# Value projections with x stationary and the weights streaming, two heads at a time

## The chip, the cores and the metric

The kernel runs on one core of a Trainium2 chip. The metric is the device time of one launch in microseconds (us), the median of the runs; lower is better. TensorE (PE) multiplies: it loads a stationary operand of 128 columns (its loads are listed as PEld) and streams a moving operand of up to 512 columns past it into PSUM. VectorE (DVE) and ScalarE (ACT) do the elementwise work, GpSimd (POOL) and SyncE (SP) mostly start transfers.

## What is computed

Two transformer layers run one after the other on 256 tokens of width 2048, in float32. The first has 16 "forgetting" softmax heads of 128 and a convolutional feed-forward part; the second has 4 heads of gated linear attention (GLA, keys of 128, values of 256) and 8 dilated softmax heads of 128, and a gated feed-forward part. Cut to the projections:

```
q, k, v, f_logit = jnp.split(h @ w_in, [hd, 2 * hd, 3 * hd], axis=-1)
q = rms_norm(q.reshape(bsz, seq, N_HEADS, HEAD_DIM), q_gain)
k = rms_norm(k.reshape(bsz, seq, N_HEADS, HEAD_DIM), k_gain)
s = jnp.einsum('bqhd,bshd->bhqs', qb, k) * scale + (cq - ck)
p = jax.nn.softmax(jnp.where(allowed, s, -jnp.inf), axis=-1)
out = jnp.einsum('bhqs,bshd->bqhd', p, v)
# second layer: qa, ka, va, ra, ga, qb, kb, vb = split(rms_norm_2(x) @ w_in)
attn = jnp.where(causal, einsum('bhnid,bhnjd->bhnij', q_t, k_t), 0.0)
o_intra = einsum('bhnij,bhnjv->bhniv', attn, vc)
chunk_state = einsum('bhncd,bhncv->bhndv', k_dec, vc)
```

So both kinds of head use v with its tokens as the contraction, that is, on the partitions.

## The kernel before

All weights arrive as 784 units of 512 KB, in the order in which they are used, through a ring of four buffers (`raw`). ACT rounds a unit to `whi` (float32r, L714), DVE takes the rest as `wlo` (L1038), three units ahead of their use (`AHEAD`). The activations stand in `xs` as a high and a low half in the same way. A unit holds 8 blocks of 128x128. For each block TensorE runs two matmuls: `whi` stationary with both halves of `xs` moving, 512 columns (L391, "hi"), and `wlo` stationary with the high half moving, 256 columns (L394, "lo"). Both add into one PSUM bank `acc`; DVE folds the two halves of the bank (`fold`, L1044) and scales them with `rstd` of the token (`take`, L1078). One chunk of 128 outputs takes two units, and comes out with features on the partitions and tokens along the row.

`stretch` writes the blocks in groups (4, 6, 6, 2 and so on): all hi matmuls of a group and then its lo ones. The order on every engine is written out by hand. `head` issues a softmax head: q into bank 1, k into bank 2, v into bank 3, six units in all; between them stand the attention steps of earlier heads: `head_values` (L453 to L455, two heads back), `head_scores` (one head back), `head_turn`. Since v must have its tokens on the partitions, `head_scores` begins with two transposes of `v_t` into the bank `b_val` (L439), and ACT copies them to `v_tok` (L745). A GLA head (`gla_head`) has twelve units: q, k, two chunks of v, two of the gate r. `gla_turn_v` transposes `g_v` in four pieces (L490), ACT copies them to `g_vtok` (L809), and only then `gla_chunk_states` (L498) can run. `b_val` also holds the transposed outputs of a GLA head (`gla_turn_out`, L510), read by DVE at L1192, which raises `g_gated`.

Waits are semaphores: `chunk_out` counts chunks that DVE has taken, `lo_ready` units that are split, `unit_used` units that TensorE is done with, `qk_rstd` and `qk_ready` the norm of q and k. A matmul that opens a bank waits for the `chunk_out` of the chunk that the bank held before.

In memory, the sizes of the tensors place every `whi` and `wlo` 128 bytes past a multiple of 256 in its partition, and `xs`, `mix` and `hid2` (the moving operands) 192 bytes past one.

Of the kernel before, what the change touches and what calls it, by code (L numbers as in the profile page):

```python
# [27 lines left out]
F32R = mybir.dt.float32r  # L28
# [6 lines left out]
P = 128  # L35
# [8 lines left out]
X_AT = 192  # L44
UW = BLOCKS * P
# [54 lines left out]
def build(nc, wstream, narrow_w, xt, vectors, identity, dist_onehot, rel_bias, gate_w2, scan_keep, gla_mask, fox_mask, out):  # L100
    with ExitStack() as ctx:
# [8 lines left out]
        whi = [sb(f"whi{i}", [P, UW], F32R) for i in range(RING)]  # L110
        wlo = [sb(f"wlo{i}", [P, UW], F32R) for i in range(RING)]
# [51 lines left out]
        v_t = put("v_t", [P, S])  # L163
        v_tok = put("v_tok", [P, 2, P])
# [26 lines left out]
        g_v = put("g_v", [P, 2, S])  # L191
# [29 lines left out]
        b_mean, b_score, b_turn, b_val = bank("b_mean"), bank("b_score"), bank("b_turn"), bank("b_val")  # L221

# [17 lines left out]
        v_turned, v_ready, scores_ready = sem("v_turned"), sem("v_ready"), sem("scores_ready")  # L240
# [6 lines left out]
        g_vturned, g_v_ready, g_cs, g_states, g_out = sem("g_vturned"), sem("g_v_ready"), sem("g_cs"), sem("g_states"), sem("g_out")  # L247
# [123 lines left out]
        def _(pe):  # L371
# [5 lines left out]

            def stretch(pos, blocks, x, *sizes):
# [3 lines left out]
                for size in sizes:  # L382
                    for k, j, bank_no, kc, opens, closes, free, late in blocks[at:at + size]:
# [4 lines left out]
                        if late:  # L388
                            pe.wait_ge(*late)
                        w_hi = whi[pos.slot(k)][:, j * P:(j + 1) * P]  # L390
                        pe.matmul(acc[bank_no][:, :], w_hi, x[:, kc, :, :].rearrange("p a s -> p (a s)"), start=opens, stop=False)  # L391
                    for k, j, bank_no, kc, opens, closes, free, late in blocks[at:at + size]:
                        w_lo = wlo[pos.slot(k)][:, j * P:(j + 1) * P]
                        mm = pe.matmul(acc[bank_no][:, S:2 * S], w_lo, x[:, kc, 0, :], start=False, stop=closes)  # L394
# [4 lines left out]
            def half(pos, k, bank_no, part, x, late=None):  # L399
                stretch(pos, unit_blocks(k, bank_no, part, None, late), x, BLOCKS)  # L400

# [48 lines left out]
            def head_values(h, means):  # L450
                pe.wait_ge(probs_t_ready, h + 1)
                pe.wait_ge(qk_rstd, means)
                pe.matmul(b_mean[:, 0:P], v_tok[:, 0, :], probs_t[:, 0:P], start=True, stop=True)  # L453
                pe.matmul(b_mean[:, P:S], v_tok[:, 0, :], probs_t[:, P:S], start=True, stop=False)  # L454
                pe.matmul(b_mean[:, P:S], v_tok[:, 1, :], probs_t[:, S:3 * P], start=False, stop=True).then_inc(head_ready, 1)  # L455
# [1180 lines left out]
```

## Time and profile before

| | us |
|---|---|
| median of the runs | 2256.49 |
| runs | 2256.23, 2256.49, 2273.54 |
| the profiled execution | 2258.64 |
| its span in the profile | 2256.9 |
| TensorE busy | 2242.0 (99%) |
| VectorE busy | 1617.8 (72%) |
| ScalarE busy | 1226.5 (54%) |

A row of a timeline gives the start, the time from the first start to the last end of a merged run of equal instructions, the engine, the line, the operation, what it writes and reads, and how many were merged; a wait stands in brackets with what ended it. Matmuls overlap in the pipe: what one of them takes of TensorE's time is the distance from its start to the start of the next, not its own duration. A row of groups gives the count, the busy time, the mean ns of one, and the idle time before. A row of waits gives who waited for whom, the us in total, how often, and the longest. A row by stretches gives the window, its length, and for each engine the busy time and (the count), then TensorE's granted clock as a share of the full one, the share of the DMA engines and GB/s.

### The profile page before, as it was taken

The page shows a single profiled execution, that of the slowest core. Times are in us where ns is not written, and L with a number is a line of the kernel's source. Part 1 is how long each engine was busy: PE and PEld are TensorE (multiplying, and loading weights), DVE is VectorE, ACT ScalarE, POOL GpSimd, SP SyncE. Part 2 cuts the span into 40 slices and gives each one's busy share as a digit, 9 for nine tenths or more (in the row PEclk, how much of TensorE's full clock was granted, in tenths as well). Part 3 has the DMA queues.
Part 4 walks back from the last instruction along what each step waited for, and adds up shares of the span by engine and source line. Part 5 has one row for each costly group of instructions (what it writes and reads, how often), then busy time and mean ns, then how long its engine had stood idle before and what let it go on. Part 6 is the DMA issues. An engine that isn't in the chain of part 4 may idle for free.

```text
span 2256.9 us, 38996 instructions
## 1 busy us (share of the span) xinstructions
PE 2242.0 (99%) x13138; PEld 1968.6 (87%) x13138; DVE 1617.8 (72%) x2394; ACT 1226.5 (54%) x1614; POOL 52.0 (2%) x78
## 2 busy tenths in 40 slices
PE   7999999999999999999999999999999999999999
PEld 6888888888888888888888888888888888888888
DVE  7877777788888888555567687777666666764554
ACT  6777765655555555444465577655444444443333
POOL 1111100000000000000000000000000000000000
PEclk9999999999999999999999999999999999999999
DMA  5555555555555555555545554455555555556564
GB/s 206 193 174 183 184 176 186 187 195 187 193 196 189 192 186 187 205 192 190 195 162 186 169 174 167 171 186 193 191 192 189 193 195 191 190 191 201 205 198 137
DMA packets 118598, 421.92 MB, mean 187 GB/s; under 512 B 13773, under 2 KB 15973, under 8 KB 118544
## 3 DMA queue, kind: packets, MB, share of 16 engines
q1 hardware_dynamic: 113760, 413.19, 53.8%
q0 software_dynamic: 2048, 5.42, 1.0%
q10 hardware_dynamic: 2736, 2.58, 0.4%
q8 instruction: 35, 0.57, 0.1%
q14 instruction: 19, 0.16, 0.0%
HBM read 419.01 MB, written 3.70 MB: 187 GB/s over the span
## 4 chain that ended last, share of the span: by engine, by line
PE 98%; DVE 1%; ACT 0%; DMA 0%; issue 0%; SPq 0%; DVEq 0%
PE acc L391 63%; PE acc L394 31%; PE b_score L442 0%; PE b_turn L447 0%; DMA xres<-xt 0%; PE b_mean L453 0%; PE b_mean L432 0%; PE b_mean L433 0%; PE b_val L439 0%; PE b_mean L455 0%; PE b_mean L454 0%; PE b_score L441 0%; ACT xs L842 0%; DVE wlo L1038 0%; DVE sq_all L1303 0%
## 5 line engine op out<-in xcount | busy, mean ns | idle before, releaser
L714 ACT ACTIVATE whi<-raw 128x1024 fp32r<-128x1024 f32 x783 | 825.8, 1058 | 821.4 <-PE acc L394 815.4
L1038 DVE TENSOR_TENSOR wlo<-raw,whi 128x1024 fp32r<-128x1024 f32 x783 | 959.5, 1229 | 389.3 <-ACT whi L714 386.6
L391 PE MATMUL acc<-xs,whi 128*128 128x512 f32 x4344 | 1130.7, 394 | 2.2 <-DVE wlo L1038 1.8
L391 PEld LDWEIGHTS acc<-xs,whi 128*128 128x128 f32 x4344 | 765.0, 188 | 124.7 <-DVE wlo L1038 2.9
L394 PEld LDWEIGHTS acc<-xs,wlo 128*128 128x128 f32 x4344 | 608.3, 188 | 64.8
L394 PE MATMUL acc<-xs,wlo 128*128 128x256 f32 x4344 | 620.3, 277 | 0.0
L391 PE MATMUL acc<-hid,whi 128*128 128x512 f32 x1408 | 359.9, 391 | 0.0
L1044 DVE TENSOR_REDUCE folded_t<-acc 128x256 f32<-128x512 f32 x336 | 231.4, 689 | 121.8 <-PE acc L394 110.2
L391 PEld LDWEIGHTS acc<-hid,whi 128*128 128x128 f32 x1408 | 247.2, 188 | 37.9
L394 PEld LDWEIGHTS acc<-hid,wlo 128*128 128x128 f32 x1408 | 194.2, 188 | 19.9
L394 PE MATMUL acc<-hid,wlo 128*128 128x256 f32 x1408 | 197.5, 276 | 0.0
L391 PE MATMUL acc<-mix,whi 128*128 128x512 f32 x512 | 131.5, 393 | 0.0
L391 PEld LDWEIGHTS acc<-mix,whi 128*128 128x128 f32 x512 | 90.4, 188 | 14.9 <-DVE mix L1136 0.5
L394 PEld LDWEIGHTS acc<-mix,wlo 128*128 128x128 f32 x512 | 70.6, 188 | 6.9
L394 PE MATMUL acc<-mix,wlo 128*128 128x256 f32 x512 | 71.9, 277 | 0.0
L830 ACT ACTIVATE hid<-hid 128x256 f32 (+1 forms) x88 | 36.2, 411 | 45.1 <-DVE hid L1265 44.9
L1104 DVE SCALAR_TENSOR_TENSOR qk_n<-qk,qk_gain,rstd_qk 128x256 f32<-128x256 f32 x48 | 21.6, 492 | 44.6 <-ACT rstd_qk L741 44.6
L1078 DVE TENSOR_TENSOR up_g<-folded_t,rstd 128x256 f32<-128x256 f32 x88 | 37.5, 426 | 3.0
L1078 DVE TENSOR_TENSOR up_v<-folded_t,rstd 128x256 f32<-128x256 f32 x88 | 37.5, 426 | 3.0
L1269 DVE TENSOR_TENSOR hid<-hid,hid 128x256 f32 (+1 forms) x88 | 36.9, 419 | 1.0 <-ACT hid L830 1.0
L815 ACT ACTIVATE tap_g<-up_g,vec 128x256 f32<-128x256 f32 x44 | 26.5, 603 | 16.2 <-DVE up_g L1078 16.1
L823 ACT ACTIVATE tap_v<-up_v,vec 128x256 f32<-128x256 f32 x44 | 26.5, 603 | 15.2 <-DVE up_v L1078 15.1
(195 smaller groups left out, 998.8 us busy)
## 6 DMA issues: line engine op xcount, KB each, us to landing
raw<-wstream SPq DMA_DIRECT2D x783, 512.0 KB, 3.3
decay_row<-decay_scratch POOLq DMA_DIRECT2D x16, 128.0 KB, 3.5
out<-xres ACTq DMA_DIRECT2D x16, 128.0 KB, 2.9
xres<-xt SPq DMA_DIRECT2D x3, 512.0 KB, 8.7
dist_scratch<-bias_scratch POOLq DMA_DIRECT2D x8, 192.0 KB, 4.7
toeplitz<-dist_scratch POOLq DMA_DIRECT2D x8, 128.0 KB, 3.3
xres<-xt SPq DMA_DIRECT2D x2, 256.0 KB, 4.6
raw<-wstream SPq DMA_DIRECT2D x2, 256.0 KB, 5.7
```

What stands on the lines that cost most here:

```text
L391: pe.matmul(acc[bank_no][:, :], w_hi, x[:, kc, :, :].rearrange("p a s -> p (a s)"), start=opens, stop=False)
L394: mm = pe.matmul(acc[bank_no][:, S:2 * S], w_lo, x[:, kc, 0, :], start=False, stop=closes)
L714: act.activation(whi[slot][:, :], raw[slot][:, :], ACT.Copy).then_inc(hi_ready, 1)
L815: act.activation(tap_g[:, :], up_g[:, 0:S], ACT.Identity, scale=column("conv0", j), bias=column("convb", j)).then_inc(tap0, 1)
L823: act.activation(tap_v[:, :], up_v[:, 0:S], ACT.Identity, scale=column("conv0", FC + j), bias=column("convb", FC + j)).then_inc(tap0, 1)
L830: act.activation(hid2[:, j, 0, :], hid[:, :], ACT.Copy).then_inc(hid_hi_ready, 1)
L1038: dve.tensor_tensor(wlo[slot][:, :], raw[slot][:, :], whi[slot][:, :], ALU.subtract).then_inc(lo_ready, 1)
L1044: dve.tensor_reduce(folded_t[0:rows, :], acc[bank_no][0:rows, :].rearrange("p (a s) -> p s a", a=2), AX_X, ALU.add).then_inc(chunk_folded, 1)
L1078: dve.tensor_tensor(dst, folded_t[0:rows, :], rstd[0:rows, :], ALU.mult).then_inc(chunk_out, 1)
L1104: dve.scalar_tensor_tensor(out=qk_n[:, a, :], in0=qk[:, a, :], scalar=qk_gain[:, col + a:col + a + 1], in1=rstd_qk[:, a, :], op0=ALU.mult, ...
L1269: dve.tensor_tensor(hid2[:, j, 1, :], hid[:, :], hid2[:, j, 0, :], ALU.subtract).then_inc(hid_split, 1)
```

## The change

The value projections swap the roles of their operands. A weight unit of values now holds 4 pieces of 256 columns (two softmax heads, or one GLA head, side by side) for 4 rows of blocks. A block is one of two 128-token halves of `xs`: its high half is stationary with the 256 columns of `whi` and of `wlo` moving, 512 columns in two runs that lie 16 KB apart (L406 of the new kernel), and its low half is stationary with `whi` moving, 256 columns (L413). Even blocks add into bank 3, odd ones into a second bank, `b_val` (bank 0 for GLA). The values come out with tokens on the partitions.

```diff
+        w = sb("w", [P, 2, RING, UW], F32R)
+        whi = [w[:, 0, i, :] for i in range(RING)]
+        wlo = [w[:, 1, i, :] for i in range(RING)]
...
+            def value_blocks(k, v, even, odd, free=None):
+                return [(k, j, (even, odd)[j % 2], (4 * v + j // 2, j % 2), v == 0 and j < 2, v == 3 and j >= 6,
+                         free if v == 0 and j == 0 else None, None) for j in range(BLOCKS)]
+            def value_parts(pos, k, j, x, kc):
+                tokens, cols = slice(kc[1] * P, (kc[1] + 1) * P), slice(j // 2 * S, (j // 2 + 1) * S)
+                return x[:, kc[0], 0, tokens], x[:, kc[0], 1, tokens], w[:, :, pos.slot(k), cols], w[:, 0, pos.slot(k), cols]
...
+            def rstd_columns(n, tile):
+                pe.wait_ge(rstd_ready, n + 1)
+                for t in range(2):
+                    mm = pe.matmul(tile[:, 2 * S - 2 + t:2 * S - 1 + t], rstd[0:1, t * P:(t + 1) * P], one[0:1, :], start=True, stop=True)
+                mm.then_inc(rstd_turned, 1)
...
             def head_scores(h):
                 pe.wait_ge(qk_ready, 2 * h + 2)
-                for t in range(2):
-                    mm = pe.transpose(b_val[:, t * P:(t + 1) * P], v_t[:, t * P:(t + 1) * P], ident[:, :])
-                mm.then_inc(v_turned, 1)
...
-            def head_values(h, means):
+            def head_values(h, means, j, taken):
+                v = slice(j * P, (j + 1) * P)
+                pe.wait_ge(chunk_out, taken)
...
-                units(8, 10, 4, 6, 6)
-                gla_turn_v(g, True)
-                units(10, 11, 4, 4)
+                units(8, 11, 4, 6, 6, 4, 4)
...
+                    elif not j:
+                        pe.wait_ge(chunk_out, chunk)
+                        pe.wait_ge(g_gated, GLA_HEADS)
...
-            def copy_v(n):
-                act.wait_ge(v_turned, n + 1)
-                act.activation(v_tok[:, :, :].rearrange("p a s -> p (a s)"), b_val[:, 0:S], ACT.Copy).then_inc(v_ready, 1)
...
+            def take_values(dst, banks, last_unit, chunk, layer):
+                dve.wait_ge(unit_used, last_unit + 1)
+                dve.wait_ge(rstd_copied, layer)
+                for t in range(2):
+                    fold(P, banks[t], chunk + t)
+                    dve.tensor_scalar(dst[:, t, :], folded_t[:, :], rstd_col[:, t:t + 1], None, ALU.mult).then_inc(chunk_out, 1)
...
                 if s == 0 and lag >= 1:
-                    take(v_t[:, :], 3, pos.unit(k0 - 1), run.chunk0 + 3 * h - 1)
+                    if not j:
+                        take_values(v_tok, (3, 4), pos.unit(k0 - 1), pair - 2, 1 if run.kind == "fox" else 2)
                     norm_qk(run, n - 1)
...
-                if s == 6:
-                    take(g_v[:, 0, :], 3, chunk(2), L1.chunk_heads + 6 * g + 2)
...
-                    take(g_v[:, 1, :], 1, chunk(3), L1.chunk_heads + 6 * g + 3)
+                    take_values(g_vtok, (3, 0), chunk(3), L1.chunk_heads + 6 * g + 2, 2)
```

The units keep their number, their size and their places; only what the value units hold is rearranged, on the host. The values of both heads of a pair are taken together, after the second head. Since a token's scale now belongs to a partition, `rstd` is turned into two columns once per layer (`rstd_columns`: two matmuls of one row and one column, and a copy by DVE). In memory, `whi` and `wlo` have become one tensor `w` that starts 224 bytes past a multiple of 256; `xs` is still at 192.

On TensorE, inside the loop over softmax heads, where a new head has issued its two q units (`b_mean` is the bank of the head outputs, `b_score` that of the scores). Before:

```order
L453 MATMUL b_mean<-probs_t,v_tok 128x128 [waits qk_rstd,probs_t_ready]
L454 MATMUL b_mean<-probs_t,v_tok 128x128
L455 MATMUL b_mean<-probs_t,v_tok 128x128
L439 MATMUL b_val<-ident,v_t 128x128 [waits qk_ready]
L439 MATMUL b_val<-ident,v_t 128x128
L441 MATMUL b_score<-qk_n 128x128
L442 MATMUL b_score<-qk_n 128x256
L385 REGISTER_ALU
L391 MATMUL acc<-xs,whi 128x512 [waits chunk_out,lo_ready]
```

After:

```order
L483 MATMUL b_mean<-probs_t,v_tok 128x128 [waits qk_rstd,probs_t_ready,chunk_out]
L484 MATMUL b_mean<-probs_t,v_tok 128x128
L485 MATMUL b_mean<-probs_t,v_tok 128x128
L469 MATMUL b_score<-qk_n 128x128 [waits qk_ready]
L470 MATMUL b_score<-qk_n 128x256
L399 REGISTER_ALU
L409 MATMUL acc<-xs,w 128x512 [waits chunk_out,lo_ready]
```

The two transposes are gone, and the head's values now wait for `chunk_out` as well.

On VectorE, where a new pair of heads begins (`folded_t` is the folded bank, `qk_n` the normed q and k). Before, for every head:

```order
L1038 TENSOR_TENSOR wlo<-raw,whi 128x1024 [waits hi_ready]
L1043 ISA [waits unit_used]
L1044 TENSOR_REDUCE folded_t<-acc 128x256 [waits chunk_out]
L1046 REGISTER_ALU
L1078 TENSOR_TENSOR v_t<-folded_t,rstd 128x256 [waits chunk_folded]
L1104 SCALAR_TENSOR_TENSOR qk_n<-qk,qk_gain,rstd_qk 128x256 [waits qk_rstd]
L1104 SCALAR_TENSOR_TENSOR qk_n<-qk,qk_gain,rstd_qk 128x256
L1037 REGISTER_ALU
L1038 TENSOR_TENSOR wlo<-raw,whi 128x1024 [waits hi_ready]
```

After, for every second head:

```order
L1065 TENSOR_REDUCE folded_t<-acc 128x256 [waits chunk_out,rstd_copied,unit_used]
L1111 TENSOR_SCALAR v_tok<-folded_t,rstd_col 128x256 [waits chunk_folded]
L1065 TENSOR_REDUCE folded_t<-b_val 128x256 [waits chunk_out]
L1111 TENSOR_SCALAR v_tok<-folded_t,rstd_col 128x256 [waits chunk_folded]
L1136 SCALAR_TENSOR_TENSOR qk_n<-qk,qk_gain,rstd_qk 128x256 [waits qk_rstd]
L1136 SCALAR_TENSOR_TENSOR qk_n<-qk,qk_gain,rstd_qk 128x256
L1059 TENSOR_TENSOR w<-raw,w 128x1024 [waits hi_ready]
```

One fold and one scaling for each head have become two and two for each pair, both ahead of the norm of q and k; the new ones write `v_tok` itself.

On TensorE, in the first dilated head, with the banks' numbers: the last unit of k and the first units of v. Before:

```order
L391 MATMUL acc2<-xs,whi3 128x512 [waits lo_ready]
L391 MATMUL acc2<-xs,whi3 128x512 x7
L394 MATMUL acc2<-xs,wlo3 128x256 x8
L391 MATMUL acc3<-xs,whi0 128x512 [waits lo_ready,chunk_out]
L391 MATMUL acc3<-xs,whi0 128x512 x7
L394 MATMUL acc3<-xs,wlo0 128x256 x8
L391 MATMUL acc3<-xs,whi1 128x512 [waits lo_ready]
```

After:

```order
L409 MATMUL acc2<-xs,w 128x512 [waits lo_ready]
L409 MATMUL acc2<-xs,w 128x512 x7
L416 MATMUL acc2<-xs,w 128x256 x8
L406 MATMUL acc3<-w,xs 128x512 [waits lo_ready,g_gated,chunk_out]
L406 MATMUL b_val<-w,xs 128x512
L406 MATMUL acc3<-w,xs 128x512
L406 MATMUL b_val<-w,xs 128x512
L406 MATMUL acc3<-w,xs 128x512
L406 MATMUL b_val<-w,xs 128x512
```

The first value matmul now waits for `g_gated` too, because `b_val`, its second bank, still holds the last GLA head's output until DVE's L1192 has read it.

## Rows read from the trace of the kernel before

**Rows 1.** The page: span, engines, and the chain that ended last.

```profile
span 2256.9 us, 38996 instructions
PE 2242.0 (99%) x13138; PEld 1968.6 (87%) x13138; DVE 1617.8 (72%) x2394; ACT 1226.5 (54%) x1614; POOL 52.0 (2%) x78
...
PE 98%; DVE 1%; ACT 0%; DMA 0%; issue 0%; SPq 0%; DVEq 0%
```

**Rows 2.** The waits of TensorE, the longest and the fourth of six.

```profile
PE acc L606 <- DVE wlo L1287: 7.4, 1, 7.4
...
PE b_mean L432 <- DVE sq_lo L1083: 0.6, 1, 0.6
```

**Rows 3.** Groups by line, shapes apart, TensorE.

```profile
L391 PE MATMUL acc<-xs,whi 128*128 128x512 f32 x4344 | 1130.7, 394 | 2.2 <-DVE wlo L1038 1.8 <-DVE xs L1061 0.4
L394 PE MATMUL acc<-xs,wlo 128*128 128x256 f32 x4344 | 620.3, 277 | 0.0
...
L439 PE MATMUL b_val<-ident,v_t 128*128 128x128 f32 x48 | 9.3, 275 | 0.0
...
L490 PE MATMUL b_val<-ident,g_v 128*128 128x128 f32 x16 | 2.4, 272 | 0.0
```

**Rows 4.** Timeline of TensorE inside one softmax head.

```profile
275.35 0.84 PE L394 MATMUL acc<-xs,wlo 128*128 128x256 f32 x6
276.03 1.54 PE L391 MATMUL acc<-xs,whi 128*128 128x512 f32 x6
277.40 0.84 PE L394 MATMUL acc<-xs,wlo 128*128 128x256 f32 x6
```

**Rows 5.** Timeline of TensorE where a head's scores are issued.

```profile
271.68 0.38 PE L439 MATMUL b_val<-ident,v_t 128*128 128x128 f32 x2
271.90 0.39 PE L441 MATMUL b_score<-qk_n 128*128 128x128 f32 x2
...
273.49 0.63 PE L394 MATMUL acc<-xs,wlo 128*128 128x256 f32 x4
273.96 0.40 PE L391 MATMUL acc<-xs,whi 128*128 128x512 f32 x1
```

**Rows 6.** Timeline of TensorE around the value transposes of a GLA head.

```profile
1245.45 0.60 PE L490 MATMUL b_val<-ident,g_v 128*128 128x128 f32 x4
1245.81 1.18 PE L391 MATMUL acc<-xs,whi 128*128 128x512 f32 x4
1246.82 0.62 PE L394 MATMUL acc<-xs,wlo 128*128 128x256 f32 x4
```

**Rows 7.** Timeline at the first dilated head.

```profile
1301.36 0.87 DVE L1192 SCALAR_TENSOR_TENSOR g_of<-b_val,vec,g_silu 128x256 f32<-128x256 f32 x2
...
1301.79 2.00 PE L391 MATMUL acc<-xs,whi 128*128 128x512 f32 x8
```

**Rows 8.** Timeline where a new pair of softmax heads begins.

```profile
284.23 0.69 DVE L1044 TENSOR_REDUCE folded_t<-acc 128x256 f32<-128x512 f32 x1 [0.87 <-PE acc L394]
...
287.25 0.88 DVE L1104 SCALAR_TENSOR_TENSOR qk_n<-qk,qk_gain,rstd_qk 128x256 f32<-128x256 f32 x2 [1.87 <-ACT rstd_qk L741]
...
289.95 0.38 PE L453 MATMUL b_mean<-probs_t,v_tok 128*128 128x128 f32 x2
```

**Rows 9.** Timeline where the output projection of the first layer begins.

```profile
322.00 0.69 DVE L1044 TENSOR_REDUCE folded_t<-acc 128x256 f32<-128x512 f32 x1 [0.77 <-PE acc L394]
...
322.73 0.42 DVE L1078 TENSOR_TENSOR v_t<-folded_t,rstd 128x256 f32<-128x256 f32 x1
...
325.13 0.88 DVE L1104 SCALAR_TENSOR_TENSOR qk_n<-qk,qk_gain,rstd_qk 128x256 f32<-128x256 f32 x2 [1.98 <-ACT rstd_qk L741]
...
325.24 0.46 PE L453 MATMUL b_mean<-probs_t,v_tok 128*128 128x128 f32 x2
```

**Rows 10.** Engines in two stretches: two forgetting heads, one GLA head.

```profile
252.08:290.00 37.92, 37.92 (x229) 33.58 (x228) 29.71 (x55) 27.07 (x42) 5.29 (x10) 1.00 0.54 183
...
1208.14:1245.46 37.32, 37.32 (x220) 32.65 (x219) 25.32 (x42) 20.90 (x26) 1.61 (x3) 1.00 0.55 179
```

More of the change, by code:

```diff
@@ L109, in build @@
         raw = [sb(f"raw{i}", [P, UW]) for i in range(RING)]
-        whi = [sb(f"whi{i}", [P, UW], F32R) for i in range(RING)]
-        wlo = [sb(f"wlo{i}", [P, UW], F32R) for i in range(RING)]
+        rstd_col = sb("rstd_col", [P, 2])
+        one = sb("one", [P, 1])
+        sb("skipped_w", [P, (W_AT - nc.sbuf_base) % PHASE // 4])
+        w = sb("w", [P, 2, RING, UW], F32R)
+        whi = [w[:, 0, i, :] for i in range(RING)]
+        wlo = [w[:, 1, i, :] for i in range(RING)]
         xres = sb("xres", [P, KC, S])
@@ L547, in project @@
                 stretch(pos, units(0, 0, 1, {0: (mix_ready, last - 1)}), mix, 4, 4)
-                head_values(last - 1, last + 1)
+                head_values(last - 1, last + 1, 0, layer.chunk_out)
                 head_scores(last)
@@ L615, in _ @@
             half(first, 3, 2, 1, xs)
-            half(first, 4, 3, 0, xs)
+            value_half(first, 4, 0, 3, 4)
             norm_mean(0)
@@ L619, in _ @@
             distance_biases()
-            half(first, 5, 3, 1, xs)
+            value_half(first, 5, 1, 3, 4)
             half(first, 6, 0, 0, xs)
             half(first, 7, 0, 1, xs)
-            pe.wait_ge(rstd_ready, 1)
+            pe.wait_ge(chunk_out, 1)
+            rstd_columns(0, b_turn)
             head_mean(0)
@@ L630, in _ @@
             head_scores(0)
-            pe.wait_ge(chunk_out, FOX.chunk0 + 3)
-            half(first, 10, 3, 0, xs)
-            half(first, 11, 3, 1, xs)
+            value_half(first, 10, 2, 3, 4)
+            value_half(first, 11, 3, 3, 4)
             head_turn(0)
@@ L1147, in head_step @@
                         dve.wait_ge(qk_ready, 2 * n)
-                    take(qk[:, 0, :], 1, pos.unit(k0 + 1), run.chunk0 + 3 * h)
+                    take(qk[:, 0, :], 1, pos.unit(k0 + 1), pair + 2 * j)
                     if lag >= 1:
@@ L1157, in head_step @@
                 if s == 4:
-                    take(qk[:, 1, :], 2, pos.unit(k0 + 3), run.chunk0 + 3 * h + 1)
+                    take(qk[:, 1, :], 2, pos.unit(k0 + 3), pair + 2 * j + 1)
                 if s == 5:
@@ L1165, in tail_step @@
                 if s == 0:
-                    take(v_t[:, :], 3, unit0 - 1, run.chunk0 + 3 * run.n - 1)
+                    take_values(v_tok, (3, 4), unit0 - 1, run.chunk0 + 3 * run.n - 2, 1 if run.kind == "fox" else 2)
                     norm_qk(run, n - 1)
@@ L1359, in first_fox_heads @@
                 square_low(0, 1)
-                take(v_t[:, :], 3, pos.unit(5), FOX.chunk0 + 2)
+                rstd_columns(1, b_turn)
                 split(10)
@@ L1562, in units_in, with units_values, units_pairs @@
     return a.reshape(-1, P, BLOCKS, P)
+def units_values(w):
+    return w.reshape(4, 4, P, 2 * P).transpose(0, 2, 1, 3).reshape(4, P, BLOCKS, P)
+def units_pairs(w, q, k, v, heads):
+    each, values = units_in(w, [c + h for h in range(heads) for c in (q, k)]).reshape(heads, 4, P, BLOCKS, P), []
+    for i in range(heads // 2):
+        u = units_values(w[:, (v + 2 * i) * P:(v + 2 * i + 2) * P])
+        values += [each[2 * i], u[:2], each[2 * i + 1], u[2:]]
+    return np.concatenate(values)
 def units_out(w):
@@ L1591 @@
     hd = FOX_HEADS * P
-    fox_order = [FOX_HEADS * part + h for h in range(FOX_HEADS) for part in range(3)]
     w1 = a["fox_w_in"][0]
```

112 lines of the change are left out of this document (63 added, 49 removed).

## The prediction

> **What bounds the kernel now.** I read the page first, then the waits of TensorE, then the groups by line, and last the timeline at the places that the change touches. The page shows TensorE busy for 2242.0 of 2256.9 us, and 98% of the chain that ended last is TensorE's [rows 1]. Its waits are few and lie at the start: the longest is 7.4 us for the first split, and one of 0.6 us for `sq_lo` stands before the first `head_mean` [rows 2]. So time is won by what leaves TensorE's stream, and lost by what enters it or makes it wait. DVE and ACT have room: in 37.92 us of two softmax heads DVE is busy 29.71 and ACT 27.07, in 37.32 us of a GLA head 25.32 and 20.90 [rows 10]. Work that only they gain or lose costs nothing unless TensorE comes to wait for it.
>
> What one matmul takes is read from starts. Six lo matmuls go from 275.35 to 276.03, 113 ns each; six hi ones from there to 277.40, 228 ns each [rows 4]. A block is 342 ns. Their own durations, 277 and 394 ns [rows 3], overlap and are no price.
>
> **The value matmuls.** There are 24 softmax heads with 2 units of values and 4 GLA heads with 4: 64 units, 512 blocks, 175 us at 342 ns. Afterwards there are as many blocks, with one load of 128 columns and 512 moving columns, one load and 256 columns, in groups of the same sizes. So the swap in itself removes no matmul. Two things in it are new. The first is that the 512 moving columns are two runs of 256. No row has such a pattern. At the low end each run costs what a 256-column matmul of its own costs, 2 x 113 = 226 ns [rows 4], 2 ns less than now: 512 x 2 = 1 us gained. At the high end I use a slower tempo that the trace knows: after the fp32 matmuls of the scores four lo matmuls go from 273.49 to 273.96, 118 ns each [rows 5]. With two runs at 118 a hi matmul would be 236 ns, 8 more, and the lo one 5 more: 512 x 13 = 6.7 us lost. I take 0, since the columns and their order within a run are the same and the row of the 256-column matmuls is the nearest. The second is that `xs` is loaded as weights and `w` streams, while DVE and ACT write other slots of `w`; they write `whi` and `wlo` today beside every load without any wait of TensorE [rows 2]. I take 0 again.
>
> **What leaves TensorE.** Two transposes per softmax head: the first of the pair starts at 271.68, the scores at 271.90, so 0.22 us [rows 5]. With 24 heads, 48 instructions [rows 3], 24 x 0.22 = 5.3 us. In a GLA head four of them run from 1245.45 to 1245.81, 0.36 us, and the four hi matmuls behind them, to 1246.82, take 1.01 where 4 x 0.228 = 0.91 would do, since their first one still waits for the last transpose in the pipe: 0.10 more [rows 6]. 4 x 0.46 = 1.8 us. Together **7.1 us** for 64 transposes.
>
> Here a rule of the Trainium skill stands against the rows. Its page "TensorE: Matmul & The Clock Gate", in the section "Part 4: PE-mode transpose", gives about 275 ns for a 128x128 transpose in a kernel's context. The trace agrees for the duration of one (272 and 275 ns), and shows about 110 from one start to the next. By the page's figure the 64 would be 17.6 us, and the sum would be 2239 us instead of the one below; this is a rival.
>
> **What enters TensorE.** The two `rstd_columns`, two small fp32 matmuls each. No row has one of one column; above, each costs no more than a transpose of 128 columns, 0.11 us [rows 5], 0.2 us per place; below, nothing. The first place lies inside the 0.6 us wait for `sq_lo` [rows 2], the second stands in the stream: I take 0.2 us, and up to 0.2 more. `head_values` gets a wait for `chunk_out` and one register instruction to compute it; I take nothing, because such instructions stand before most groups today without a wait in the rows.
>
> **New waits.** In the first dilated head the first value matmul waits for `g_gated`. It is due at 1301.79, but DVE's L1192 runs from 1301.36 for 0.87 us, to 2.23 [rows 7]. TensorE waits about **0.5 us**, once; all that is queued behind it, the other value blocks and the `head_mean` of that head, comes later by as much, and since TensorE sets the end, so does the end.
>
> The other waits are for the values. In the loop DVE folds at 284.23; the norm of q and k can start only at 287.25, when `rstd_qk` is there [rows 8]. A fold and its scaling take from 322.00 to 323.15, 1.15 us [rows 9]; two pairs take 2.3 us and end at 286.5, 0.7 us before DVE can go on anyway. The head's values on TensorE are due at 289.95 [rows 8], 3.4 us after. The tightest place is the start of the output projection, where only one unit lies between: DVE folds at 322.00, would be done at 324.3, and the norm starts at 325.13, just ahead of the values at 325.24 [rows 9], which wait for the same `rstd_qk`. So the cover is 0.8 us there. If it went, TensorE would wait for the rest of the second pair, at most 1.1 us at each of 12 pairs. In a GLA head the two pairs come where one is now, two units further on than a fold that goes away; their reader, `gla_chunk_states`, follows three units later (8 us). What ACT no longer does, 28 copies, hides behind TensorE and brings nothing.
>
> **The sum.** The profiled execution took 2258.64 us, 1.7 more than its span and 2.1 more than the median. 2258.6 - 7.1 + 0.5 + 0.2 = 2252.2; against the median, 2256.5 - 6.4 = **2250 us**, 0.3% less.
>
> **Rivals.**
>
> *Every matmul becomes slower (slower than before).* The change also moves the weights of all 6264 blocks [rows 3] from 128 to 224 bytes past a multiple of 256. If a load then takes longer, the lo matmul, which has the least time to hide the next load, shows it first. For it: lo matmuls do run at 118 instead of 113 in places [rows 4, 5], so something other than their 256 columns can hold them. Against it: no row ties that to an address. Price: 5 ns for each block would be 6264 x 5 = 31 us, less those that are slow today; with some 6000 it is 30, and 2250 + 30 = 2280 us. It decides from about 1 ns per block, 6.4 us, where the gain is gone. The same page, section "LDWEIGHTS (loading the stationary operand)", gives a load as its columns over 1.2 GHz, 107 ns for 128; by it a lo matmul, 113 ns here, has hardly any room for a longer load. It states nothing on addresses, and no row here shows that a load sets this pace.
>
> *The two runs cost something (no change).* The high end above: +6.7, so 2256 to 2257 us, with the transposes paid back. For it, the pattern is new to this kernel; against it, its reads are still whole runs of 1 KB.
>
> *TensorE waits for the values.* The wait of the transposes is replaced by one for DVE: 12 x 1.1 = 13 us at most, 2263 us. Against it stand covers of 0.7 us and more at DVE and 3.4 us at TensorE [rows 8, 9].
>
> *Transposes cost their whole duration, or the new placement helps.* By [rows 3] 48 x 0.275 + 16 x 0.272 = 17.6 us: 2258.6 - 17.6 + 0.7 gives 2242 for the profiled execution, 2239 or 2240 against the median. Against it, the rows of starts. A placement that took 2 ns from each hi matmul would give 6264 x 2 = 13 us: 2237 us. Nothing in the rows asks for it.
>
> **Chances.** Forecast 0.66 (its own range 2245 to 2255: the tempo after fp32 matmuls, 113 or 118, varies between heads, and 0.15 us for each of 24 heads is 4 us); two runs dearer 0.12; waits for values 0.05; all matmuls slower 0.10; cheaper in one of the last two ways 0.07. The range reaches from 2240 to 2270: it holds the forecast, the dearer runs and the waits, and the lower half of the slower matmuls; it leaves out some 0.06 on each side. A change of 1% (23 us, below 2234 or above 2279) is about what a measurement can tell from none. Faster by more has 0.03, slower by more 0.06, within it 0.91.
>
> **What would show it right or wrong.** Starts of six hi matmuls of values 1.37 us apart as a group, and six lo ones 0.68: the swap is free. No row with `v_t` or `g_v`, and the scores right behind the head's values: the transposes are gone, 0.22 us a head. One wait of TensorE for DVE's `g_of` near 0.5 us: the new wait. No waits of TensorE for `v_tok` or `g_vtok`: the cover holds. The q and k groups, and the feed-forward parts that the change does not touch, at 1.37 and 0.68 as now: if these are longer, the first rival holds, and the prediction is wrong by tens of us.

## The result: 2% slower, in all matmuls on the streamed weights

The changed kernel takes 2306.92 us (median; 2306.75 to 2308.92) where the kernel before, run beside it, takes 2257.39: a ratio of 1.0187, with a 95% interval of 1.0137 to 1.0236. The forecast was 2250. The profiled execution took 2306.75 us and has a span of 2305.0, 48.1 more than before. Executions of one and the same kernel can differ by steps of some 13 us (the kernel before: 2256 to 2260, 2270 to 2274, seldom 2283), and the last section of the experiments follows one such step in two profiles.

The page of the changed kernel, the lines that answer to [rows 1]:

```profile
span 2305.0 us, 38875 instructions
PE 2289.7 (99%) x13082; PEld 1996.3 (87%) x13082; DVE 1619.4 (70%) x2397; ACT 1217.9 (53%) x1586; POOL 52.0 (2%) x78
...
PE 98%; ACT 1%; DMA 1%; DVE 1%; issue 0%; SPq 0%; DVEq 0%
```

TensorE has 56 matmuls fewer and is busy 47.7 us longer. Its waits, the view of [rows 2]:

```profile
PE acc L629 <- DVE w L1321: 7.1, 1, 7.1
PE acc L409 <- DVE w L1059: 1.8, 1, 1.8
PE b_mean L463 <- DVE sq_lo L1115: 1.1, 1, 1.1
...
PE acc L406 <- issue: 0.3, 1, 0.3
```

None of them is new and long. So the 48 us are in the stream itself. Where [rows 4] and [rows 5] were read, two q and k groups, a value group and the scores now stand like this on the timeline of TensorE:

```profile
271.22 0.39 PE L484 MATMUL b_mean<-probs_t,v_tok 128*128 128x128 f32 x2
271.44 0.39 PE L485 MATMUL b_mean<-probs_t,v_tok 128*128 128x128 f32 x2
271.66 0.39 PE L469 MATMUL b_score<-qk_n 128*128 128x128 f32 x2
271.89 0.60 PE L470 MATMUL b_score<-qk_n 128*128 128x256 f32 x2
...
275.84 1.56 PE L409 MATMUL acc<-xs,w 128*128 128x512 f32 x6
277.23 0.88 PE L416 MATMUL acc<-xs,w 128*128 128x256 f32 x6
277.95 0.39 PE L406 MATMUL acc<-w,xs 128*128 128x512 f32 x1
...
279.35 0.28 PE L413 MATMUL acc<-w,xs 128*128 128x256 f32 x1
...
280.05 0.39 PE L406 MATMUL acc<-w,xs 128*128 128x512 f32 x1
```

Six hi matmuls of q and k take 277.23 - 275.84 = 1.39 us, six lo ones 0.72 (before 1.37 and 0.68 [rows 4]); six value ones 1.40 and 0.70. The lo matmuls, at 120 ns instead of 113, are the clearest sign. The slower pace is also where the change altered nothing. In the feed-forward part of the first and of the second layer, TensorE's matmuls in 300 us, first before, then after (window, length, busy and count, clock, DMA share, GB/s):

```profile
600.00:900.00 300.00, 300.00 (x1755) 1.00 0.56 191
1800.00:2100.00 300.00, 300.00 (x1755) 1.00 0.57 195
```

```profile
600.00:900.00 300.00, 300.00 (x1705) 1.00 0.56 186
1800.00:2100.00 300.00, 300.00 (x1706) 1.00 0.56 187
```

A block is two matmuls: 300 / 877.5 = 341.9 ns before, 300 / 852.5 = 351.9 after, at the same granted clock (1.00, the level of 2.4 GHz). (A window also counts the matmuls that its two ends cut, so these figures are 0.3 ns low in a window of 300 us; from start to start they are 342.2 and 352.2.)

Now all starts of the two traces, with each block compared with the block of the same unit. The 5760 blocks that kept their form (the first unit's included) went from 231.2 to 234.2 ns behind a hi matmul and from 115.1 to 120.8 behind a lo one, 8.7 ns a block and 49.9 us in all. The 512 value blocks went from 350.0 to 355.2 ns, 2.7 us. All other matmuls, the transposes among them, take 71.9 us before and 67.6 after (4.2 less, unrounded), and the first matmul starts 0.3 us earlier. 49.9 + 2.7 - 4.2 - 0.3 = 48.1, the whole difference of the spans.

### The profile page after: what moved, and what is told of

Its sections match the earlier page's. It is cut to its first block, busy times and chain, and to the rows that moved or that the text cites. A ratio compares the mean times of both kernels' runs of the same rounds, so it can differ in the third digit from the quotient of the medians.

```text
span 2305.0 us, 38875 instructions
## 1 busy us (share of the span) xinstructions
PE 2289.7 (99%) x13082; PEld 1996.3 (87%) x13082; DVE 1619.4 (70%) x2397; ACT 1217.9 (53%) x1586; POOL 52.0 (2%) x78
## 4 chain that ended last, share of the span: by engine, by line
PE 98%; ACT 1%; DMA 1%; DVE 1%; issue 0%; SPq 0%; DVEq 0%
PE acc L409 58%; PE acc L416 30%; PE acc L406 3%; PE b_val L406 2%; PE acc L413 2%; PE b_val L413 1%; PE b_score L470 0%; PE b_turn L475 0%; DMA xres<-xt 0%; PE b_mean L463 0%; PE b_mean L483 0%; PE b_score L469 0%; PE b_mean L464 0%; PE b_mean L485 0%; PE b_mean L484 0%
## 5 line engine op out<-in xcount | busy, mean ns | idle before, releaser
L746 ACT ACTIVATE w<-raw 128x1024 fp32r<-128x1024 f32 x783 | 824.9, 1057 | 872.8 <-PE acc L416 827.5
L1059 DVE TENSOR_TENSOR w<-raw,w 128x1024 fp32r<-128x1024 f32 x783 | 959.3, 1228 | 419.8 <-ACT w L746 417.5
L409 PE MATMUL acc<-xs,w 128*128 128x512 f32 x3832 | 1005.0, 397 | 2.2 <-DVE w L1059 1.8
L409 PEld LDWEIGHTS acc<-xs,w 128*128 128x128 f32 x3832 | 680.4, 188 | 119.8 <-DVE w L1059 2.9
L416 PEld LDWEIGHTS acc<-xs,w 128*128 128x128 f32 x3832 | 548.2, 188 | 59.1
L416 PE MATMUL acc<-xs,w 128*128 128x256 f32 x3832 | 565.4, 282 | 0.0
L409 PE MATMUL acc<-hid,w 128*128 128x512 f32 x1408 | 364.9, 394 | 0.0
L409 PEld LDWEIGHTS acc<-hid,w 128*128 128x128 f32 x1408 | 249.2, 188 | 41.4
L416 PEld LDWEIGHTS acc<-hid,w 128*128 128x128 f32 x1408 | 200.6, 188 | 21.1
L416 PE MATMUL acc<-hid,w 128*128 128x256 f32 x1408 | 206.8, 283 | 0.0
L409 PE MATMUL acc<-mix,w 128*128 128x512 f32 x512 | 133.2, 396 | 0.0
L406 PE MATMUL acc<-w,xs 128*128 128x512 f32 x320 | 111.3, 401 | 0.3 <-issue 0.3
L409 PEld LDWEIGHTS acc<-mix,w 128*128 128x128 f32 x512 | 91.0, 188 | 16.0 <-DVE mix L1168 0.5
L416 PEld LDWEIGHTS acc<-mix,w 128*128 128x128 f32 x512 | 72.5, 188 | 7.3
L406 PE MATMUL b_val<-w,xs 128*128 128x512 f32 x192 | 75.9, 395 | 0.0
L406 PEld LDWEIGHTS acc<-w,xs 128*128 128x128 f32 x320 | 58.8, 188 | 10.2 <-issue 1.1
L413 PE MATMUL acc<-w,xs 128*128 128x256 f32 x320 | 67.6, 280 | 0.0
L413 PEld LDWEIGHTS acc<-w,xs 128*128 128x128 f32 x320 | 54.0, 188 | 5.5
```

The costliest lines, as they stand in the source:

```text
L406: pe.matmul(acc[bank_no][:, :].rearrange("p (a s) -> p a s", a=2), x_hi, w_both, start=opens, stop=False)
L413: mm = pe.matmul(acc[bank_no][:, S:2 * S], x_lo, w_hi, start=False, stop=closes)
L746: act.activation(whi[slot][:, :], raw[slot][:, :], ACT.Copy).then_inc(hi_ready, 1)
L1059: dve.tensor_tensor(wlo[slot][:, :], raw[slot][:, :], whi[slot][:, :], ALU.subtract).then_inc(lo_ready, 1)
```

## Experiments

What is common to q, k, output and feed-forward matmuls is where their weights lie. The theories (the expectations call form and rest together theory B):

- **Placement.** `w` at 224 instead of 128 (places are bytes past a multiple of 256) slows every matmul. Either its own place counts (A1), or the distance from the stationary to the moving operand (A2), or how ACT and DVE write into `w` while TensorE reads (A3).
- **Form.** The new value blocks, with two runs and alternating banks, leave the pipe in a slower state that lasts.
- **The rest.** The dropped transposes, the new tensors or semaphores change the pace.

From here on *distance* is the place of the moving operand minus that of the stationary one, modulo 256. Before it was 192 - 128 = 64 for every block. After it is 192 - 224 = 224 for the old blocks, and 224 - 192 = 32 for the value blocks, where the roles are swapped.

### The kernel before with its weights at 224

```diff
+        sb("pad_w", [P, 24])
         whi = [sb(f"whi{i}", [P, UW], F32R) for i in range(RING)]
         wlo = [sb(f"wlo{i}", [P, UW], F32R) for i in range(RING)]
+        sb("pad_x", [P, 40])
```

> The kernel before, with 96 bytes of padding ahead of the rounded weights, so that every whi and wlo starts 224 bytes past a multiple of 256 as in the changed kernel, and padding behind them so that xres and xs keep 128 and 192. Nothing else differs. Theory A (the start of the weights in the partition makes every block slower, wherever it is used): six hi and six lo matmuls take 2.10 us and more instead of 2.05, and the time is 2300 to 2315 us, since the changed kernel lost 50 us and saved some 6 elsewhere. Theory B (the swap of operands, the alternating banks or the new code slow TensorE down, the placement is innocent): 2257 us as before.

2313.5 us (2313.32 and 2313.67), ratio 1.0218 [1.0160, 1.0276]. Two empty tensors do it. Its groups of lo and hi in the second feed-forward part, and its matmuls in the same two windows:

```profile
1800.44 1.56 PE L393 MATMUL acc<-xs,whi 128*128 128x512 f32 x6
1801.83 0.88 PE L396 MATMUL acc<-xs,wlo 128*128 128x256 f32 x6
1802.55 0.62 PE L393 MATMUL acc<-xs,whi 128*128 128x512 f32 x2
```

```profile
600.00:900.00 300.00, 300.00 (x1705) 1.00 0.57 186
1800.00:2100.00 300.00, 300.00 (x1705) 1.00 0.58 187
```

1.39 and 0.72 us for six, and 1705 matmuls: the pace of the changed kernel, with no value block in it. Theories of form and of the rest fall as causes of the 48 us. The span is 2311.9, 55.0 above before and 6.9 above after. Run times alone would leave the ratio uncertain (the 13 runs of the kernel before beside it go from 2256.32 to 2283.28); the paces in the traces do not depend on that.

### The changed kernel with its weights at 128, and at 192

```diff
-        sb("skipped_w", [P, (W_AT - nc.sbuf_base) % PHASE // 4])
+        sb("skipped_w", [P, 48])
```

> The changed kernel with w at 128 past a multiple of 256, where whi and wlo stood before. Theory A: 2251 us, 6 less than before, because then only the forecast terms are left: 7.1 us for the transposes, 0.5 and 0.2 for the new wait and the columns. Theory B: near 2307, as the changed kernel. If the two runs of 256 moving columns cost something themselves, up to 7 us more than 2251.

2255.85 us (2254.46 to 2269.68, 10 runs), ratio 0.9982 [0.9952, 1.0013]. For the second, `skipped_w` is 64 columns, and `skipped` also, so that `xs` stays at 192:

> The changed kernel with w at 192, the place that the constant W_AT names. Theory A1 (a load is slow when it starts 32 bytes past a multiple of 64): as fast as with 128, 2251 us. Theory A2 (what counts is how the stationary and the moving operand stand to each other within 256 bytes: 64 apart before, 32 after): here they are 0 apart, and the time differs from that with 128 by more than 10 us, most likely upwards. Theory B: 2307.

2294.69 us (2293.76 to 2296.06), ratio 1.0135 [1.009, 1.018]. The two windows, at 128 and then at 192:

```profile
600.00:900.00 300.00, 300.00 (x1756) 1.00 0.59 190
1800.00:2100.00 300.00, 300.00 (x1757) 1.00 0.61 194
```

```profile
600.00:900.00 300.00, 300.00 (x1716) 1.00 0.58 187
1800.00:2100.00 300.00, 300.00 (x1715) 1.00 0.59 189
```

At 128, the place before, the loss of 48 us is gone, and the feed-forward blocks are at 341.6 ns again. The gain that was expected, down to 2251 us, does not come in full. At 192 (distance 0) a block takes 349.7. At 192 the value blocks run at the pace of the q and k blocks, 231.3 and 118.7 ns for both (median of the groups of six): two runs of 256 columns and two alternating banks cost nothing there. At 128 they run at 233.8 and 115.2, where the median group of the old blocks has 228.8 and 113.3; the swap of the roles turns their distance from 64 to 192. By these medians that would be 6.9 ns x 512 = 3.5 us, the price from which the experiment with the values at distance 64 starts. Start to start and unit by unit it is less: the value blocks took 350.0 ns in the kernel before, slower than its feed-forward blocks, and take 353.3 here, 3.3 more or 1.7 us.

### The kernel before with xs moved, alone and together with the weights

```diff
-X_AT = 192
+X_AT = 224
```

> The kernel before with the weights left at 128 and the moving operands xs, mix and hid2 at 224 past a multiple of 256. Theory A1, which is about loads only: 2257 us. A form of it in which any operand that starts 32 bytes past a multiple of 64 is slow: 2290 to 2310. Theory A2 (distance between the two, now 96): also slower, by an amount that it doesn't say. Theory B: 2257.

2321.48 us, ratio 1.0253 [1.0195, 1.0312]: distance 96, the slowest of all kernels here. The weights lie where they lay, and what ACT and DVE write into them is the same; A1, which is about the stationary operand's place, falls as the only cause, and A3 with it. Next, the weights at 224 as in the first experiment and `X_AT = 32`, so both lie 96 bytes on and the distance is 64 again:

> The kernel before with both moved by the same 96 bytes: weights at 224 past a multiple of 256, xs, mix and hid2 at 32 (224 + 64). Theory A2 (only the distance from the stationary to the moving operand counts, modulo 256 bytes): 2257 us, blocks at 228.8 and 113.3 ns, as before. Theory A1 (an operand 32 bytes past a multiple of 64 is slow by itself): 2310 us or more, since now both are. Theory A3 (it is the writes of ScalarE and VectorE to w, by their place, that hold TensorE): also about 2310, since the weights are where they were in the slow run.

2258.01 us (8 runs, 2256.31 to 2285.63) against 2258.84: 0.9997 [0.9950, 1.0043]. The windows of the second feed-forward part, distance 96 and then 64:

```profile
1800.00:2100.00 300.00, 300.00 (x1701) 1.00 0.57 186
```

```profile
600.00:900.00 300.00, 300.00 (x1721) 1.00 0.56 188
1800.00:2100.00 300.00, 300.00 (x1757) 1.00 0.60 193
```

352.7 ns a block against 341.5. The same `w` at 224 that cost 55 us costs nothing once `xs` goes along: it is the distance (A2). The 1721 in the first layer is taken up below.

### TensorE alone: maps of the distance

The first map holds only TensorE's blocks (six hi, six lo, four times) for all 64 pairs of places in steps of 32 bytes, on operands that nobody writes:

> No part of the reference is computed: after one load and one rounding, TensorE alone runs 64 stretches of 24 hi and 24 lo matmuls in groups of six, one for each pair of places (stationary and moving operand at 0, 32, ... 224 past a multiple of 256), with a small fp32 matmul between stretches; ScalarE, VectorE and the transfers rest. Theory A2: the pace depends on moving minus stationary alone, 228.8 and 113.3 ns at +64, 232.2 and 120.0 at -32, 231.3 and 118.7 at 0, 233.2 and 120.2 at +96, the same along each diagonal. Theory A1: rows and columns at 32, 96, 160, 224 are slow and the others fast. Theory A3: all 64 stretches run at 229 and 113, since nobody else touches the memory.

A group of hi and one of lo, stationary at 128, moving at 192 and then at 224:

```profile
394.00 1.55 PE L68 MATMUL acc<-x,w 128*128 128x512 f32 x6
395.38 0.87 PE L70 MATMUL acc<-x,w 128*128 128x256 f32 x6
396.09 0.40 PE L68 MATMUL acc<-x,w 128*128 128x512 f32 x1
...
402.54 1.57 PE L68 MATMUL acc<-x,w 128*128 128x512 f32 x6
403.94 0.52 PE L70 MATMUL acc<-x,w 128*128 128x256 f32 x3
```

1.38 us against 1.40 for the six hi ones, with all other engines idle: no other engine is needed for a difference. Neither map computes anything of the reference. The second map adds moving places up to 1 KB on, steps of 16 bytes, and the form of the value blocks with two alternating banks and with one:

> No part of the reference is computed: TensorE alone, as in the first map, but with the lo weights 16 KB behind the hi ones as in the kernel, the stationary operand at 128 and the moving one at 0 to 992 in steps of 32, then at 144 to 256 in steps of 16; then 8 stretches in the form of the values (tokens stationary at 192, two runs of 256 columns moving at 0 to 224, two banks in turn) and 8 of that form with one bank. Theory A2 with a period of 256 bytes: the four rounds of the first 32 repeat each other, the best is +64, and there the pace is 228.8 and 113.3. The value form: the same paces at the same distance, 228.8 and 113.3 for the moving operand at 0, 231.2 and 118.7 at 192, 233.8 and 115.2 at 128, with one bank as with two.

Mean distances of starts in ns, hi / lo, by the distance of the operands, the first group of each stretch left out; first map (mean of eight pairs), value form of the second map with two banks and with one (one pair each, the stationary at 192):

```
distance      0            32           64           96           128          160          192          224
first map     231.2/118.8  232.3/117.5  230.3/118.0  234.0/119.3  231.9/117.2  233.2/117.6  232.4/115.2  232.9/119.4
two banks     230.6/118.7  231.6/117.3  228.8/117.7  233.2/120.2  231.7/117.1  232.9/117.4  232.3/117.9  232.2/120.0
one bank      230.6/118.7  231.5/117.3  228.8/117.7  233.2/120.2  231.7/117.1  233.0/117.3  232.3/117.9  232.2/120.0
```

At six of the eight distances the pace repeats with 256 bytes: with the stationary at 128, moving places 192, 448, 704 and 960 (distance 64) all give 230.8 / 118.1, and 64, 320, 576 and 832 (distance 192) all give 232.5 / 114.2. The form of the value blocks costs nothing, and neither does their bank pattern: at the same pair of places, with the stationary at 192, the first map and the two value rows agree within 0.1 ns for hi and 0.3 for lo (moving at 0: 228.8 ns for hi in all three, so 230.3 in the table is the mean of unlike pairs). Distances 96 and 224 are worst, as in the kernels, with 353.3 to 353.6 and 352.1 to 352.4 ns a block in all eight pairs of each.

But the distance alone does not set the pace, as the expectation of the first map had it. Within one distance the pairs differ: a block takes 349.3 to 353.5 ns at distance 0, 346.7 to 349.0 at 64, 346.7 to 350.0 at 192. Nor do the two places settle it: the pair 128 and 160 stands twice in the second map, with 351.1 and 348.7, so what ran before counts too. And no block at distance 64 came near the 342.2 of the kernels; no group of lo matmuls reached 113.3 there. From 64 to 224 the maps have 3 to 6 ns a block, the kernels 10. The last experiment takes this up.

### Values at distance 64 too

Each slot of `w` is 64 columns longer, and value units are written and read 128 bytes on, so that their place is 0 and their distance 0 - 192 = 64:

```diff
+V_AT = 32
-        w = sb("w", [P, 2, RING, UW], F32R)
+        w = sb("w", [P, 2, RING, UW + 64], F32R)
...
-                act.activation(whi[slot][:, :], raw[slot][:, :], ACT.Copy).then_inc(hi_ready, 1)
+                act.activation(w[:, 0, slot, unit_at(pos.base + k)], raw[slot][:, :], ACT.Copy).then_inc(hi_ready, 1)
```

> The changed kernel with w at 128 and, in addition, the value units written 128 bytes further on in their slots, so that for values too the moving operand (w, at 0 modulo 256) stands 64 above the stationary one (xs, at 192). Theory A2 (only moving minus stationary counts): value groups of six fall from 233.8 and 115.2 ns (run with w at 128) to 228.8 and 113.3, 6.9 ns for each of 512 blocks, 3.5 us less than that run: 2251 us, 6 less than before. If the two runs of 256 columns or the alternating banks have a price of their own, the value groups stay above 229 and 113, and the time at 2254.

2268.18 us (2255.98 to 2283.21, 12 runs), ratio 1.0043 [1.0011, 1.0075]: not the gain of 3.5 us. Start to start the value blocks went from 353.3 to 352.0 ns, 1.3 less, 0.7 us in all (lo matmuls at 117.4, not 113.3), and the first layer's feed-forward part runs slow, the second's not:

```profile
600.00:900.00 300.00, 300.00 (x1722) 1.00 0.58 188
1800.00:2100.00 300.00, 300.00 (x1757) 1.00 0.60 194
```

### The transposes issued twice

```diff
-                for t in range(2):
+                for t in (0, 1, 0, 1):
```

in `head_scores` and, the same, in `gla_turn_v` of the kernel before: 64 more transposes (the repeated ones write the same results again).

> The kernel before with each of the 64 value transposes issued twice. By the distances between starts, 0.22 us a head and 0.45 us a GLA head, it takes 7.1 us more than before (64 x 0.11); by the rule of 275 ns for one, 17.6 us more.

2267.77 us (10 runs) where the kernel before beside it has a median of 2257.00, ratio 1.0016 [0.9987, 1.0045]. The 23 runs of the kernel before go from 2255.87 to 2283.62, so the times do not resolve 7 us; the traces do. The span is 2267.5, 10.6 above before. On the timeline:

```profile
51.00 0.60 PE L439 MATMUL b_val<-ident,v_t 128*128 128x128 f32 x4
51.43 0.39 PE L441 MATMUL b_score<-qk_n 128*128 128x128 f32 x2
```

Four take 0.43 us where two took 0.22 [rows 5]. Over all places, the time from the matmul ahead to the one behind grows from 342.3 to 560.5 ns in a softmax head and from 474.2 to 911.2 in a GLA head: 24 x 0.218 + 4 x 0.437 = 7.0 us, 109 ns each. The wait for `sq_lo` is 1.4 us longer, and most of the remaining 2 us are head blocks at a slower pace: of the groups of six lo matmuls in the first 330 us, 65 of 84 run near 118 ns, where in the kernel before it was 26 of 85. So the transposes' own price is that of the prediction, 7.1, and not 17.6.

### Two tempi at distance 64

Two profiles have a slow first layer: that of the kernel before with both operands moved, and that with the values at distance 64. The changed kernel with `w` at 128 was run once more, the same code:

> The changed kernel with w at 128 once more, for a closer ratio. If the change without its placement is worth the 2.7 us that the two profiled executions are apart: 0.9988 of the kernel before. If it is nothing: 1.000. A gain of 0.3% as forecast (0.997) needs the values' blocks to cost nothing, which the earlier run of it does not show (6.9 ns a block, 3.5 us).

2255.08 us (12 runs), ratio 0.9981 [0.9959, 1.0003]. This time the profiled execution was one of the longer ones, span 2267.6 against 2254.2:

```profile
600.00:900.00 300.00, 300.00 (x1724) 1.00 0.55 188
1800.00:2100.00 300.00, 300.00 (x1755) 1.00 0.56 194
```

348.0 ns a block in the first layer's feed-forward part (348.9 from start to start), where the earlier profile of this kernel has 341.7 (342.2). Laid side by side, the two traces are 0.3 us apart at 492 us and 13.4 at 1209, and from there to the end the difference stays 13.5. So at distance 64 there are two tempi, hi 228.9 / lo 113.3 and hi 230.8 / lo 118.1 ns (the next expectation leaves out the last matmul of each group and so has 228.4 and 231.2), and in these two traces the loop of the first feed-forward part keeps one of them throughout. Is that TensorE's own doing too?

> TensorE alone again, nothing of the reference is computed. At the distance of the kernel before (stationary 128, moving 192) the kernels' own traces show two tempi, hi 228.4 with lo 113.4 ns and hi 231.2 with lo 118 ns, and they go from the one to the other in the first half. Stretches of 60 to 160 groups of hi and lo matmuls: groups of six at that distance without a break, the same with the stationary at 224, with a 128-column matmul after every group, after every fourth, the same in float32, groups of 4, 6, 6, groups of 8, the stationary at 224 with a float32 matmul after every fourth, and the first one again. If the quick tempo is the state that an undisturbed stream finds and a break throws it out of it, the first and last stretch run at 228.4 and 113.4 after some groups, those with breaks at 231 and 118 for some groups behind each, and the stretches at 224 stay at 232 and 120 throughout. If the quick tempo needs the other engines' traffic, all stretches at 192 run at 230 and 118 as in the map of 64 combinations. If only float32 matmuls bring the slow tempo, the fifth stretch alone shows it.

TensorE alone at distance 64, in a long stretch of groups of six ahead and in one at the end that has the same instructions; between them a stretch at distance 224:

```profile
200.00:380.00 180.00, 180.00 (x1040) 1.00 0.00 1
420.00:500.00 80.00, 80.00 (x457) 1.00 0.00 1
...
1520.00:1660.00 140.00, 140.00 (x822) 1.00 0.00 1
```

From start to start a block takes 346.7 ns in the first (228.8 / 117.8), 342.2 in the last (228.9 / 113.3) and 352.2 at distance 224; the counts of such short windows would make it up to 2 ns less. No engine but TensorE is at work. The last stretch is quick from its first group, the first never becomes quick in its 160 groups. With a float32 matmul behind every fourth group, the tempo changes at the break:

```profile
889.36 0.87 PE L79 MATMUL acc<-x,w 128*128 128x256 f32 x6
890.07 0.38 PE L68 MATMUL mark<-xraw,wraw 128*128 128x128 f32 x2
...
891.68 0.84 PE L79 MATMUL acc<-x,w 128*128 128x256 f32 x6
892.36 1.54 PE L77 MATMUL acc<-x,w 128*128 128x512 f32 x6
...
898.52 0.38 PE L68 MATMUL mark<-xraw,wraw 128*128 128x128 f32 x2
...
900.13 0.87 PE L79 MATMUL acc<-x,w 128*128 128x256 f32 x6
900.84 1.55 PE L77 MATMUL acc<-x,w 128*128 128x512 f32 x6
```

Six lo matmuls take 0.71 us ahead of the first break, 0.68 behind it and 0.71 behind the next; two stretches at 118 and one at 113 follow each other regularly. With a 128-column matmul of the rounded operands as a break, all stay at 117 to 118. Groups of eight, without a break, alternate between 118 and 113, and those of 4, 6, 6 go three by three. At distance 224 float32 breaks never bring the quick tempo: 118 right behind one and 120 after it. So each of my expectations is wrong in part: the quick tempo needs no other engine, a stream of groups of six does not find it by itself, and more than float32 matmuls can change it. What went before sets the tempo; by what means is not shown, and what sets it in the kernel, ahead of the first layer's feed-forward part, is open.

This also splits the 10.0 ns that a feed-forward block lost in the changed kernel. At distance 64 a block takes 342.2 ns at the quick tempo and 348.9 at the slow one; at 224 it takes 352.2, and not one group of lo matmuls in the changed kernel is below 115 ns (889 of 1029 groups of four or more are in the kernel before). So 6.7 ns are the quick tempo, which distance 224 never showed, and 3.3 ns are what 224 costs on top of the slow one.

## Why the prediction was wrong, step by step

- **What bounds the kernel: right.** 98% of the chain is TensorE's, and what was slow was slow in its stream.
- **The pace of the blocks that keep their form: this step failed.** The sum has terms for transposes, columns and one wait, and leaves all other blocks at their old pace; the move of the weights from 128 to 224 stands in it at nothing, with no row that says so. The runs show 8.7 ns a block by all starts (10.0 in the feed-forward parts), 49.9 us: the distance between the operands went from 64 to 224. The placement stood among the rivals, with 0.10, and its price was too small, 5 ns a block and 31 us. I had priced the lo matmuls alone (5.7 by all starts), and the hi ones became 3.0 ns slower as well. The sign named for this rival, q and k groups and feed-forward parts longer than 1.37 and 0.68, is the one that came: 1.39 and 0.72. The mechanism that I gave it, a longer load by the weights' own place, is refuted: at the same 224 with `xs` at 32 nothing is lost. That lo matmuls run at 118 in places was rightly seen as a sign that something besides their columns holds them; it is the slow tempo of distance 64. The evidence against the rival, "no row ties that to an address", said that nothing was known, and I read it as a small chance. The range ended at 2270 for that reason.
- **The value blocks: nearly.** "Two runs cost nothing" is shown by the kernel at distance 0 and by the second map. "I take 0 again", for `xs` as weights and `w` streaming, is wrong by a little: it was argued from the writes of ACT and DVE and the absence of waits [rows 2], but the swap turns the distance round. Against the blocks of the same units before, that is 1.7 us with `w` at 128 and 2.7 us in the changed kernel itself.
- **The transposes: right.** No row of `v_t` or `g_v`, and the scores start 0.22 us behind the last matmul of the head's values. The doubled transposes measure 7.0 us for 64. By the Trainium skill, "TensorE: Matmul & The Clock Gate", section "Part 4: PE-mode transpose", a transpose takes about 275 ns, and an estimate by it for the doubling is 17.6 us; the trace agrees with the 275 as a duration (272 and 275 ns [rows 3]) and not as a price in a stream (109 ns).
- **`g_gated`: right.** DVE's L1227 is late by this much, shown on the timeline of the changed kernel:

```profile
1324.94 0.87 DVE L1227 SCALAR_TENSOR_TENSOR g_of<-b_val,vec,g_silu 128x256 f32<-128x256 f32 x2
...
1325.91 0.47 PE L406 MATMUL acc<-w,xs 128*128 128x512 f32 x1 [0.26 <-issue]
```

  The row shows 0.26 us of idle time; counted from starts, the first value matmul comes some 0.4 us later than the pace of the lo matmuls ahead of it would have it, for the forecast 0.5.
- **`rstd_columns`: too small.** Its two matmuls are four instructions in the trace, not two. At the second place they hold TensorE from 1174.06 to 1174.53, 0.47 us, where 0.2 and at most 0.4 were allowed:

```profile
1174.06 0.60 PE L430 MATMUL b_mean<-one,rstd 1*128 1x1 f32 x4
1174.53 1.10 PE L673 MATMUL b_score<-ga,w_sb 16*128 16x256 f32 x4
```

  At the first place the wait for `sq_lo` hides them. That wait itself says nothing of them: it is 1.1 us here, but 1.7 in the kernel before with `w` at 224, which has no columns, and absent in the changed kernel with values at distance 64, which has them.
- **The covers of the values: right.** No wait for `v_tok` or `g_vtok` in the list.
- **The sum without the placement.** With `w` at 128 the two profiles of the quick tempo are 2254.2 and 2256.9, 2.7 us apart where the prediction had 6.4. By starts, the blocks that keep their form take the same (1994.8 us in both), the value blocks 1.7 us more, all other matmuls 4.2 us less, and the first matmul starts 0.2 us earlier. In the 4.2 are the 6.8 us of the transposes' own starts, less 2.4 for the columns; 2.0 of these stand at the first place, and 1.4 of them are the wait for `sq_lo`, which in the kernel before (0.6) counts with the block ahead of it. The two sets of runs give 0.9982 and 0.9981, with intervals that end at 1.0013 and 1.0003. A gain of 0.2% is likely and not proven. That version is the best one found.

How `w` came to 224, by the places that the program assigns, counted past a multiple of 256 (no trace holds addresses): `one` ends at 164, and the filler is computed from there for 192, 28 bytes. But the places assigned are multiples of 32. So the filler starts at 192 and ends at 220, and `w` starts at 224. The fillers of the two experiments agree with this: 192 bytes from 192 on lead to 128, and 256 bytes to 192. Even at 192, as was meant, the kernel would have been slow (2294.69).

## What to carry to other kernels

When an edit adds, removes or merges tensors, work out where the operands of the busiest matmuls come to lie, to 256 bytes, and how far the stationary is from the moving one; if the distance changes, set it back with a filler first and time the rest after that. Read the places from what the program assigns, since a filler computed for one place can land at another. Where operands swap roles, the distance changes its sign. Count matmuls in a window far from the edit in both traces: if they differ there, the cause is not the edit's own work. And a rival on which the rows are silent deserves a chance for what isn't known, above all when it multiplies by all blocks of the kernel.

## What was new about the hardware

- The pace of float32r matmuls that stream past a stationary operand depends on the distance of the two in the partition, modulo 256 bytes: 341.5 to 352.7 ns for a block of 512 + 256 columns in these kernels, 3%, at an unchanged granted clock. With all other engines idle it depends on it too (342.2 ns at the quickest and 352.2 at distance 224 in one run).
- The distance is not all of it. At distance 64 there are two tempi, 228.9 / 113.3 and 230.8 / 118.1 ns, and other distances showed more than one pace as well (349.3 and 353.5 ns a block at 0). What went before sets which one it is, and the loop of a feed-forward part kept it for 700 us. This is the source of 13.4 us between two executions of the same code; the still longer executions near 2283 us were not seen in a profile.
